# Differential attention: where the two rounds of transposes and the value products stand in a step of TensorE's program

## What is computed

```python
def diff_causal_attention(q, k, v, lam):      # q,k: (B,H,2,S,64); v: (B,H,S,128); H = 4, S = 1024
    for j in range(S_ // Q_BLOCK):            # Q_BLOCK = 128: eight query blocks
        lo, hi = j * Q_BLOCK, (j + 1) * Q_BLOCK
        s = jnp.einsum('bhmqd,bhmkd->bhmqk', q[:, :, :, lo:hi], k[:, :, :, :hi]) * scale
        mask = jnp.arange(hi)[None, :] <= jnp.arange(lo, hi)[:, None]
        p = jax.nn.softmax(jnp.where(mask, s, -jnp.inf), axis=-1)
        pd = p[:, :, 0] - lam * p[:, :, 1]
        outs.append(jnp.einsum('bhqk,bhkd->bhqd', pd, v[:, :, :hi]))
```

## Time and profile before

| what | value |
|---|---|
| runs | 3539.45, 3536.3, 3539.17 us; median 3539.17 us |
| the profiled execution: its own time | 3537.67 us |
| its span in the profile | 3535.9 us |
| TensorE matmul / weight load busy | 3348.6 us (95%) / 2688.9 us (76%) |
| VectorE / ScalarE / GpSimd busy | 1360.8 us (38%) / 760.3 us (22%) / 1192.8 us (34%) |
| chain that ended last, by engine | PE 84%, DVE 10%, ACT 3%, issue 2%, POOL 1% |
| chain, by line | L451 50%, L485 17%, L516 4%; L860 and L877 1% each |
| mean granted TensorE clock over the span | 0.97 |

### The profile page before, as it was taken

One profiled execution on the slowest core, in us unless ns is written; L12 is line 12 of the kernel. 1 busy time (PEld: TensorE's weight loads), 2 busy tenths in 40 slices (PEclk: granted clock), 3 DMA queues, 4 the chain that ended last, 5 costly groups with the idle time before them and its releaser, 6 DMA issues.

```text
span 3535.9 us, 37512 instructions
## 1 busy us (share of the span) xinstructions
PE 3348.6 (95%) x15576; PEld 2688.9 (76%) x15576; DVE 1360.8 (38%) x1653; ACT 760.3 (22%) x1108; POOL 1192.8 (34%) x992
## 2 busy tenths in 40 slices
PE   7999989999898999999999999998997999999997
PEld 5577767888685688788888888887865688888886
DVE  5265073331505503233331111237997652222223
ACT  4230164221205401112110000023442311001001
POOL 5212300354330233344443433342321344444441
PEclk9989999999898999999999999998998999999998
DMA  4111100021210011121111111112111111111111
GB/s 184 36 42 42 48 1 25 24 92 64 101 48 13 16 51 58 44 96 49 38 58 48 47 47 48 48 48 78 36 60 48 36 48 48 47 47 47 47 48 48
DMA packets 32333, 181.72 MB, mean 51 GB/s; under 512 B 3920, under 2 KB 4944, under 8 KB 15312
## 3 DMA queue, kind: packets, MB, share of 16 engines
q1 hardware_dynamic: 19936, 139.99, 11.2%
q10 hardware_dynamic: 12272, 39.89, 3.0%
HBM read 164.15 MB, written 15.73 MB: 51 GB/s over the span
## 4 chain that ended last, share of the span: by engine, by line
PE 84%; DVE 10%; ACT 3%; issue 2%; POOL 1%; DMA 0%; DVEq 0%; ACTq 0%; SPq 0%; POOLq 0%
PE ps L451 50%; PE ps L485 17%; PE ps L516 4%; PE ps L2128 3%; DVE c_out L2577 3%; PE ps L1631 1%; PE ps L860 1%; PE ps L1647 1%; PE ps L733 1%; PE ps L2150 1%; PE ps L2204 1%; DVE p L1824 1%; PE ps L1617 1%; PE ps L742 1%; PE ps L877 1%
## 5 line engine op out<-in xcount | busy, mean ns | idle before, releaser
L573 POOL TENSOR_TENSOR whi<-raw,par 128x512 fp32r<-128x512 f32 x116 | 128.1, 1104 | 1952.9 <-PE ps L451 1424.5
L577 POOL TENSOR_TENSOR wlo<-raw,whi 128x512 fp32r<-128x512 f32 x464 | 688.3, 1483 | 37.0
L451 PE MATMUL ps<-xhi,whi 128*128 128x512 f32 x2016 | 631.0, 394 | 27.9 <-DVE xlo L346 7.7
L451 PE MATMUL ps<-xlo,whi 128*128 128x512 f32 x2016 | 626.3, 392 | 0.0
L451 PE MATMUL ps<-xhi,wlo 128*128 128x512 f32 x2016 | 624.3, 391 | 0.0
L451 PEld LDWEIGHTS ps<-xhi,whi 128*128 128x128 f32 x2016 | 379.0, 189 | 111.4 <-issue 13.0
L451 PEld LDWEIGHTS ps<-xlo,whi 128*128 128x128 f32 x2016 | 381.8, 189 | 81.2
L451 PEld LDWEIGHTS ps<-xhi,wlo 128*128 128x128 f32 x2016 | 381.1, 189 | 81.4
L575 POOL CAST whi<-raw 128x512 fp32r<-128x512 f32 x348 | 285.4, 820 | 0.0
L485 PE MATMUL ps<-hidden_hi,whi 128*128 128x512 f32 x864 | 268.5, 392 | 0.4 <-DVE hidden_lo L1487 0.4
L485 PE MATMUL ps<-hidden_lo,whi 128*128 128x512 f32 x864 | 268.9, 393 | 0.0
(11 more groups left out here) (487 smaller groups left out, 4580.7 us busy)
## 6 DMA issues: line engine op xcount, KB each, us to landing
raw<-stream SPq DMA_DIRECT2D x131, 1024.0 KB, 4.8
x_again<-xT ACTq DMA_DIRECT2D x4, 1024.0 KB, 8.3
h_scr<-x_again ACTq DMA_DIRECT2D x4, 1024.0 KB, 4.4
h<-h_scr ACTq DMA_DIRECT2D x1, 4096.0 KB, 15.6
h_scr<-h ACTq DMA_DIRECT2D x4, 1024.0 KB, 4.4
outT<-h ACTq DMA_DIRECT2D x8, 512.0 KB, 3.0
bias<-bias ACTq DMA_DIRECT2D x1, 2560.0 KB, 9.1
x_in<-xT ACTq DMA_DIRECT2D x2, 1024.0 KB, 17.4
```

What stands on the lines that cost most here:

```text
L451: mm = nc.tensor.matmul(ps[:, c0 + c:c0 + c + width], w, x(k, a, width), start=(n == 0 and m == 0), stop=(n == len(ks) - 1 and m == 2))
L573: nc.gpsimd.tensor_tensor(WHI[:, r, t], RAW[:, r, t], one, ALU.mult).then_inc(hi_done, 1)
L577: ins = nc.gpsimd.tensor_tensor(WLO[:, r, t], RAW[:, r, t], WHI[:, r, t].bitcast(F32), ALU.subtract)
```

## The change

Only the order within an iteration of TensorE's program changes. The first round of transposes of step i - 2 moves from behind the scores of step i to ahead of them, with its wait for `d_p`. The second round of step i - 2 moves from behind the value products of step i - 3 to ahead of them. The value products come last. No instruction, tile or semaphore is added or taken away, and the programs of the other engines stay as they are.

```diff
             for i in range(n_steps + 3):
+
+                if 2 <= i < n_steps + 2:
+                    pe.wait_ge(S("d_p"), i - 1)
+                    transposes(i - 2, 0)
                 if i < n_steps:
 
                     h, j = STEPS[i]
...
                     for m in range(2):
                         e = scores_at(i, m) + n - P
                         nc.tensor.matmul(ps[:, e:e + P], IDR[:, :], MKR[:, :], start=False, stop=True).then_inc(S("d_scores"), 1)
-                if 2 <= i < n_steps + 2:
-                    pe.wait_ge(S("d_p"), i - 1)
-                    transposes(i - 2, 0)
+                if 2 <= i < n_steps + 2 and ROUNDS[i - 2] == 2:
+                    transposes(i - 2, 1)
                 if i >= 3:
                     s, (h, j) = i - 3, STEPS[i - 3]
                     c = BANK * 7
...
                         mm = nc.tensor.matmul(ps[:, c:c + P], PTD[s % 2][:, P * k:P * (k + 1)],
                                               VD[:, k, P * h:P * (h + 1)], start=(k == 0), stop=(k == j))
                     mm.then_inc(S("d_o"), 1)
-                if 2 <= i < n_steps + 2 and ROUNDS[i - 2] == 2:
-                    transposes(i - 2, 1)
```

## The result

The changed kernel takes 3565.85 us in the median of four runs (3565.18 to 3573.26), the kernel before 3538.20 us on the same chip (four runs). The ratio is 1.0081, with a 95% interval from 1.0068 to 1.0093: slower, as forecast, and by 27.65 us where 17 to 18 were forecast. The time lies at the upper end of the range.

The account below looks back on a forecast made before the run. The prediction took a chain passing from engine to engine (scores, minimum, exponential) as the bound. Head terms 5.2 + 4.4 + 4.2 + 3.8 - 0.2 gave +17.4 us on 3537.67, taken as 3556 us, range 3547 to 3567.

Parts of the forecast that it names:

- The mechanism: In the stage, transposes ahead of the scores wait for a late combination; alone this gives +12 to +22 us.
- A long step: A step of 1024 columns behind one of 896 takes 5.58 us, where it was 4.80: +0.78.
- that chain: Through ScalarE: exponential, copy of the second round emptying bank 6, then next first round; 5.77 us at most.
- The turns: Short steps behind a long one: step 8 loses 1.1 us, the two behind it take 3.06 and 3.15 us.
- The sum: Whole stage: heads 0 to 3 lose 5.2, 4.4, 4.2 and 3.8, last iterations -0.2; together +17.4 us.
- the case of no more half clock: TensorE in the stage: the sum as worked out, ending at 3556 us, chance 0.70.
- the case with one or two more stretches: Rival: emptier TensorE stretches fall to half clock, 3.3 us each; +20 to +25, 3558 to 3564 us, chance 0.22.
- Second round: Waits for ScalarE's first-round copy, holding up the values; free where scores are long, step 8 loses 1.1 us.
- No change: Rival: transposes hidden by a sooner combination, or short steps gain what long ones lose; +6, 3544 us, chance 0.05.
- faster: Rival: ScalarE's 15.7 us of waiting for the transposes is given back in full; 3522 us, chance 0.03.

Follow-up runs that it names:

- making the two inputs early: Changed kernel with VectorE's combination ahead of the first minimum and ScalarE's second-round copy ahead of the first exponential: 3541.80 us, ratio 1.0008.
- the early combination: Changed kernel with VectorE combining step i - 1 ahead of the first minimum of step i: 3555.72 us, ratio 1.0047.
- the run with the early copy alone: Changed kernel with ScalarE's copy of the second round ahead of the first exponential, combination late as before: 3569.17 us, ratio 1.0082.
- the run with the filling: Changed kernel with unused identity products in TensorE's idle time, ahead of the combination wait and, in steps 8 and 16, the second round: 3559.26 us, ratio 1.0059.
- taking them away by the filling: Kernel before with unused identity products ahead of the stage and of the scores of steps 1 to 6: 3536.86 against 3539.01 us, ratio 0.9994.

## Why the prediction was right, and by how much it was off

- **The mechanism.** The combination is made too late for transposes ahead of the scores, and the chain scores, minimum, combination, transposes takes the place of scores, minimum, exponential. Shown: the waits changed places as forecast, and making the two inputs early took the stage from 150.8 to 128.7 us with TensorE's order unchanged. Either one alone took less than 0.1 us off steps 6, 7 and 25 (the early combination made step 6 0.2 longer). VectorE's wait for the mask product grew from 24.1 to 48.1 us, and the values of step 8 started 2.95 us behind its scores, both as forecast.
- **A long step.** Forecast 5.58 us, measured 5.72. The 0.14 is two small terms: 0.15 us went by from the end of the combination to the transposes, not 0.10, and 0.55 us from the start of the transposes to that of the scores (465.72 to 466.27), not 0.46. The 0.15 is not VectorE's alone: ScalarE's copy ends at the same 465.57, and where the copy had long been done the transposes went 0.05 to 0.06 us behind the combination (466.10 to 466.16 in the run with the early copy alone). Step 15, where the copy ended last, took 5.83 us, slightly more than the 5.77 that the prediction gave as the most for that chain.
- **The turns.** Step 8 was forecast at 5.07 and is 4.81 in the run with the filling; step 9 takes 3.13 us there, forecast 3.06. The small gain behind each turn is real (3.46 to 3.13 in step 9, 3.24 to 2.91 in step 17); step 10 took 3.27, forecast 3.15.
- **The sum.** +17.4 was for TensorE's clock as before the change. With the clock as before, measured: +19.2 with the filling, +18 without what the filling costs. By heads, with the filling: head 0 +4.7, head 1 +4.8, head 2 +4.7, forecast 5.2, 4.4 and 4.2; head 3, which has no stretch at half clock in the changed kernel, +4.0 there, forecast 3.8. The three rising heads miss by up to 0.5 each, two up and one down, so a little of the agreement of the sum is luck.
- **What was mis-sized: the clock.** The mechanism without it, worked out to 3556 us, falls 10 us short of the measured 3565.85. That time is 1.15 us below the end of the range at 3567, which was drawn for half clock, and one run of the four (3573.26) lies above it: that the range held owes something to luck. The prediction took the case of no more half clock as the likeliest, at 0.70, and the case with one or two more stretches at 0.22. What came had four new stretches and a longer first one: head 1 lost 6.4 us where 4.4 were forecast, head 2 10.5 where 4.2 were. That case's place was right (the emptied steps of the rising heads), its count too low. The price was about right in short steps: 3.3 us for the 12.86 us of the early steps is 0.26 for each us, and taking them away by the filling gave back 3.15. In the long steps of heads 1 and 2 it is higher, 7.4 us (1.6 and 5.8) for the 17.1 us of the four new stretches, by the same two heads with the filling: 0.43 for each us. More of TensorE's own time stands on the path there (14 products 3.20 us instead of 1.73); that this is the reason is an argument, not shown by a run. The Trainium skill's rule (TensorE: Matmul & The Clock Gate, Terms), half of the throttled time, would be an estimate of 8.5 us for those 17.1 and 6.4 for the early steps; both measurements lie below it.
- **Second round.** I priced it at the turns alone. By itself it costs 12.4 us. Beside the moved first round it costs nothing at the same clock: the stage with the first round alone would be some 144.4 us (148.4 less the 4 for half clock), that of the changed kernel some 142.4 (143.7 with the filling, less what the filling costs). These two are estimates from the steps. What it did cost in these traces is clock, four new stretches against two.
- **No change and faster.** Both fell where the prediction said they would be decided: the combination ended behind the exponential (465.57 against 465.20).

What stays open: how much of the changed kernel's time differs from run to run through the place of the stretches at half clock. The four runs spread over 8 us (3565.18 to 3573.26), those of the kernel before over 3 (3536.30 to 3539.45), and there is a trace of one of each. Which emptied stretch is followed by half clock also stays open.

## What to carry to other kernels

Idle time ahead of a wait is no free place for work that needs a later input: before moving an operation forward, look up in the timeline when each of its inputs is ready, and compare that with the end of the wait it is meant to hide in. An order by hand is a property of all engines together; the order that lost 26 us in the stage lost 4 when the two that feed it were reordered to match. And a change that empties TensorE can have a second price, half clock in the steps behind.

## What the runs showed that I had not expected

Products that no one uses made the changed kernel 6.6 us faster (3565.85 to 3559.26), by the clock alone. The two moves cost 23.9 and 12.4 us alone and 26.4 together. One late input hid another: in steps 6, 7 and 25 either early input by itself was worth less than 0.1 us, and both together 0.6 to 0.7. The wait for the combination by itself cost 3.4 us (some 5 at the same clock), less than half of what I had expected at most; by difference the transposes behind it cost most of the rest.
